# A triangular inverse on four quarters of TensorE's array, in pairs behind half units, and another order at the end of softmax

## The chip, the cores and the metric

The kernel runs on one core of a Trainium2 chip. The metric is the time of one execution on the device in microseconds (us), lower being better. Each engine (TensorE or PE, VectorE or DVE, ScalarE or ACT, GpSimd or POOL, SyncE or SP, which issues the weight DMAs) has its own queue and works it off in order. Engines wait for each other by semaphores.

## What is computed

One transformer block over 256 tokens of width 2048: a gated feed-forward, a mixer with two branches, and a second feed-forward, each with a layer norm. All is float32.

```
h = layer_norm(DEEPNORM_ALPHA * h + 0.5 * swiglu(h, ffn1_w_gate[l], ffn1_w_up[l], ffn1_w_down[l]), ...)
mix = hybrid_mixer(h, w_in[l], ...)
h = layer_norm(DEEPNORM_ALPHA * h + mix, ln2_g[l], ln2_b[l])
h = layer_norm(DEEPNORM_ALPHA * h + 0.5 * swiglu(h, ffn2_w_gate[l], ffn2_w_up[l], ffn2_w_down[l]), ...)
```

The mixer projects h by `w_in`. One branch is sparse attention: latent queries are projected by `w_q_idx` (for the index that picks 64 keys for each query) and by `w_uq` (for the attention), and softmax follows over the picked keys. The other is a gated delta rule over 8 heads in chunks of 64 tokens:

```
a_mat = jnp.where(strict, jnp.einsum('bhncd,bhned->bhnce', k_beta, k) * decay, 0.0)
m_mat = a_mat + jnp.eye(CHUNK, dtype=a_mat.dtype)
value = solve(v_beta)             # solve: a triangular solve with m_mat
k_cumdecay = solve(k_beta * jnp.exp(g_cum)[..., None])
```

The kernel solves by building the inverse of `m_mat`: 4 chunks of 64 tokens, 8 heads.

## The kernel before

**Units.** Every large product is cut into units: a 256 x 512 piece of a weight matrix. SP loads it into `raw` (8 slots), ACT rounds it into `whi` (`split_hi`, L351), DVE computes the rest into `wlo` (`split_lo`, L358), and `unit_mm` on PE multiplies with both. `whi` and `wlo` have 3 slots; a slot is free when the semaphore `unit_used` says that PE has finished the unit that used it, and PE raises `unit_used` behind the unit's last matmul only. ACT and DVE split unit w+2 while PE is at unit w. With the slot order of `ring_place`, which turns back in the second half of a product's units so that the next product finds its slots in order, the 8 units of `w_q_idx` take slots 0, 1, 2, 0, 1, 0, 1, 2 and the 4 of `w_uq` slots 0, 1, 2, 1. So units 5 and 6 take the slots of units 3 and 4, and unit 11 that of unit 9: these splits can only start when the unit two before them is finished.

**The latent query stage.** 12 units (w = 0 to 11) of 24 matmuls at L393, L395, L397, moving 256 columns each. A unit has two halves of 12 matmuls, one for each bank of `acc0`. Behind every second unit ACT evicts `acc0` into `qidxT` or `qT` (L1308).

**The inverse.** A tile has 128 partitions, and each of the two tiles of 128 tokens (t = 0, 1) holds two chunks, one on partitions 0 to 63 (`UPPER`), one on 64 to 127 (`LOWER`). The inverse Y and its transpose X grow over five levels: `t1_mm` (L1952) multiplies a level's part of the matrix with X, ACT evicts it to `t1` (L1317); `y_mm` (L1965) multiplies `t1` with Y, DVE subtracts it from Y (`yinv`, L1644, at level 5 into `yfull`, L1648); `x_mm` (L1978) transposes Y into X, ACT evicts it to `xinv` (L1321). A sixth step (L1955, L1968) joins the two chunks of a tile. Each of the steps is one *group* for each t: 8 heads x 2 chunks = 16 matmuls of 64 x 64, which the profile shows as 32 records, since a float32 matmul is two passes. A matmul whose operands are on `UPPER` and whose output is on `UPPER` uses one quarter of the 128 x 128 array, `LOWER` to `LOWER` the opposite one. The other two quarters are not used. The groups run as `items_behind(w)` between units: six (t1, y and x of a level, both t) behind each of the units 1, 3, 5 and 7, four each behind 8 and 9, two behind 10. `split_hi` and `split_lo` stand ahead of an even unit's groups and behind an odd unit's. PSUM: X and t1 in `acc1`, Y's product in two banks of `tp`.

**Behind it** come the index scores, the choice of 64 keys on DVE, the softmax on DVE and ACT (`logits`, `select`, `exps`, `normalise`), and beside it on PE the products of the delta rule: `vnew0`, `nkcd` (evicted by DVE, L1751), the state, o0 (L2095, which waits for `nkcd`'s eviction, since it overwrites its bank and the state's later product reads it), `vnew1`, then the attention's outputs `oT` (L2121 to L2123, one head after another through four banks; head h waits until `oT_lo` has read head h-4, L1784), then the units of `w_out`.

Of the kernel before, what the change touches and what calls it, by code (L numbers as in the profile page):

```python
# [19 lines left out]
P = 128  # L20
# [91 lines left out]
def hybrid_block(nc, x, x_t, ffn1_w_gate, ffn1_w_up, ffn1_w_down, ln1_g, ln1_b, w_in, q_norm_g, kv_norm_g,  # L112
# [52 lines left out]
    with ExitStack() as ctx:  # L165
# [209 lines left out]
        def unit_mm(pe, p, it, u, acc, free, n_chunk, moving, stat, kt0, first, last, a_done=None):  # L375


            n = st.phases[p].units
            s = ring_place(u, n, SPLIT_SLOTS)
            pe.wait_ge(lo_done, st.index(p, it, u + 1))  # L380
            for half in range(2):
                if first and n_chunk is not None:
                    wait(pe, free[half], n_chunk)
                if moving == "w":
                    ins = token_mm(pe, p, it, u, acc, half, stat, kt0, first, last)
                else:
                    for c in range(2):
                        cols = slice((2 * half + c) * P, (2 * half + c) * P + P)
                        o = acc[:, half, c * S:c * S + S]
                        for k in range(UNIT_KT):  # L390
                            hi, lo = stat[:, kt0 + k, 0, :], stat[:, kt0 + k, 1, :]
                            end = last and k == UNIT_KT - 1
                            pe.matmul(o, whi[:, s, k, cols], hi, start=first and k == 0 and c == 0,  # L393
                                      stop=False, skip_group_check=True)
                            pe.matmul(o, whi[:, s, k, cols], lo, start=False, stop=False,  # L395
                                      skip_group_check=True)
                            ins = pe.matmul(o, wlo[:, s, k, cols], hi, start=False, stop=end,  # L397
                                            skip_group_check=True)
                if half == 0 and last and a_done is not None:
                    ins.then_inc(a_done, 1)  # L400
            ins.then_inc(unit_used, 1)
# [514 lines left out]
        QUARTERS = (UPPER, LOWER)  # L916
        NAMES = ["xa", "ax", "spl", "sp", "beta", "tb", "g", "eg", "ekd", "gc", "rq", "rk",
# [45 lines left out]
        def x_bank(t):  # L963
            return acc1[:, t]

        def y_bank(t):
            return tp[:, t]
# [11 lines left out]
        def items_behind(w):  # L979
            return range(*{1: (0, 6), 3: (6, 12), 5: (12, 18), 7: (18, 24), 8: (24, 28), 9: (28, 32), 10: (32, 34)}.get(w, (0, 0)))  # L980

        def y_ups(lvl, t):

            done = T * (lvl - 1) + t + 1
            return done + (t + 1 if lvl == LEVELS else T if lvl > LEVELS else 0)
# [175 lines left out]
        def mixer_act(act):  # L1161
# [129 lines left out]
            def x_first(t):  # L1291

                act.wait_ge(sem("x0_ps"), t + 1)
                act.activation(xinv[:, t], heads8(x_bank(t)), ACT.Copy).then_inc(sem("x0"), 1)

            x_first(0)
            for w in range(LATENT_UNITS):
                p, u = latent_stage(w)
                if w % 2 == 0:
                    split_hi(act, p, 0, u + LEAD)  # L1300
                if u % QU == QU - 1:
                    j, dst = u // QU, (qidxT if p == WQI else qT)
                    for half in range(2):
                        if half == 0:
                            act.wait_ge(acc0a_done, n0[p] + j + 1)
                        else:
# [3 lines left out]
                if w == 0:  # L1310
                    x_first(1)
                for m in items_behind(w):
                    lvl, kind, t = item(m)
                    if kind == 0:
                        act.wait_ge(sem("t1_ps"), T * (lvl - 1) + t + 1)
                        rows = slice(0, P) if lvl <= LEVELS else LOWER
                        act.activation(t1[rows, t], heads8(x_bank(t)[rows]), ACT.Copy).then_inc(sem("t1"), 1)  # L1317
                    if kind == 2:
                        act.wait_ge(sem("x_ps"), T * (lvl - 1) + t + 1)
                        rows = slice(0, P) if lvl < LEVELS else UPPER  # L1320
                        act.activation(xinv[rows, t], heads8(x_bank(t)[rows]), ACT.Copy).then_inc(sem("x_up"), 1)  # L1321
# [53 lines left out]
            act.wait_ge(sem("o_out"), 1)  # L1375
            act.activation(o_squares[:, 0], o_first[:], ACT.Square).then_inc(sem("o_sq"), 1)
# [20 lines left out]
            for h in range(AH):  # L1397
                oT_hi(h)
                if h == 5:
                    act.wait_ge(sem("o_sum"), 2)  # L1400
                    act.activation(o_squares[:, 1], o_second[:], ACT.Square).then_inc(sem("o_sq"), 1)
# [27 lines left out]
        def mixer_dve(dve):  # L1429
# [203 lines left out]
            for w in range(LATENT_UNITS):  # L1633
                p, u = latent_stage(w)
                if w % 2 == 0:
                    split_lo(dve, p, 0, u + LEAD)
                if w == 0:
                    qk_times_decay(3)
                for m in items_behind(w):
                    lvl, kind, t = item(m)  # L1640
                    if kind == 1:
# [4 lines left out]
                        elif lvl == LEVELS:  # L1646
                            for rows in QUARTERS:
                                dve.tensor_tensor(yfull[rows, t, :, rows], yinv[rows, t], heads8(y_bank(t)[rows]),  # L1648
                                                  ALU.subtract).then_inc(sem("y_up"), 1)
# [3 lines left out]
                if w % 2:  # L1653
                    split_lo(dve, p, 0, u + LEAD)
# [63 lines left out]
            def select(i):  # L1718
# [6 lines left out]
                   .then_inc(sem("att_sel"), 1)  # L1725
                dve.wait_ge(sem("att_sel"), i + 1)
                dve.reduce_max(amax[:, t, heads], prob, AX_X).then_inc(sem("att_max"), 1)
                dve.wait_ge(sem("att_max"), i + 1)
# [67 lines left out]
            o_mean_square(0)  # L1796
            second_queries(2)
# [3 lines left out]
            for h in range(4):  # L1801
                oT_lo(h)
# [3 lines left out]
            for h in range(4, AH):  # L1806
                oT_lo(h)
            dve.wait_ge(sem("o_sum"), 2)
# [23 lines left out]
        def mixer_pe(pe):  # L1832
# [98 lines left out]
            def x_first(t):  # L1931
# [3 lines left out]
                for h in range(BH):  # L1935
                    for rows in QUARTERS:
                        ins = pe.matmul(x_bank(t)[rows, cols64(h)], yinv[rows, t, h], ident[rows, rows],
# [3 lines left out]
            def t1_mm(lvl, t):  # L1941
# [3 lines left out]
                if lvl == 1:  # L1945
                    pe.wait_ge(sem("x0"), t + 1)
                else:
                    pe.wait_ge(sem("x_up"), T * (lvl - 2) + t + 1)
                for h in range(BH):
                    if lvl <= LEVELS:  # L1950
# [3 lines left out]
                    else:  # L1954
                        ins = pe.matmul(x_bank(t)[LOWER, cols64(h)], aT[UPPER, t, h, LOWER], xinv[UPPER, t, h],  # L1955
# [3 lines left out]
            def y_mm(lvl, t):  # L1959

                pe.wait_ge(sem("t1"), T * (lvl - 1) + t + 1)
                for h in range(BH):
# [9 lines left out]
            def x_mm(lvl, t):  # L1972

                pe.wait_ge(sem("y_up"), y_ups(lvl, t))
                for h in range(BH):
                    if lvl < LEVELS:
                        for rows in QUARTERS:
                            ins = pe.matmul(x_bank(t)[rows, cols64(h)], yinv[rows, t, h], ident[rows, rows],  # L1978
                                            start=True, stop=True)
                    else:  # L1980
                        ins = pe.transpose(x_bank(t)[UPPER, cols64(h)], yfull[UPPER, t, h, UPPER], ident[UPPER, UPPER])
# [23 lines left out]
            for w in range(LATENT_UNITS):  # L2005
                p, u = latent_stage(w)
                j = u // QU
                unit_mm(pe, p, 0, u, acc0, acc0_free, n0[p] + j, "x", cqT, 2 * (u % QU), u % QU == 0, u % QU == QU - 1,
                        acc0a_done)
                if w == 0:  # L2010
                    x_first(1)
                for m in items_behind(w):
                    lvl, kind, t = item(m)
                    (t1_mm, y_mm, x_mm)[kind](lvl, t)
# [231 lines left out]
```

## Time and profile before

| | |
|---|---|
| median of 3 runs | 1948.9 us (1948.44 to 1949.24) |
| the profiled execution, its own time | 1949.24 us |
| its span | 1947.4 us |
| latent query stage (first matmul at L393 with `cqT` to first score matmul) | 989.34 to 1059.45 us |
| from the scores to the first unit of `w_out` | 1059.45 to 1113.02 us |

A matmul's record starts when the array takes it; its duration holds a latency of some 0.2 us in which others run, so the distance from start to start is what PE needs. A row with "x64" is a run of 64 records; its start and the start of the next row give the run's time. "Idle before <- who" is the time in which an engine had nothing in flight and who ended it. PE can look busy while it loses time: a late start of 0.1 to 0.2 us is hidden under the latency of the record ahead.

### The profile page before, as it was taken

To read this page: it belongs to the slowest core of one execution; us is meant where nothing else is said; L and a number is where in the kernel's file an instruction comes from. 1 tells how busy PE (TensorE), PEld (TensorE's weight loads), DVE (VectorE), ACT (ScalarE), POOL (GpSimd) and SP (SyncE) were. 2 spreads that over 40 slices of the span, in tenths; PEclk is the share of its full clock that TensorE was granted. 3 is DMA by queue.
4 is the path that set the end of the run, shared out by engine and by line. 5 is a ranking of instruction groups with operands and counts; after the bars stand their busy time and mean duration, and the time that the engine had idled before them with its cause. 6 is when DMAs were issued, how large, how long until landed. Compare 5 with 4: busy or idle time off the path is not lost.

```text
span 1947.4 us, 28504 instructions
## 1 busy us (share of the span) xinstructions
PE 1930.1 (99%) x10574; PEld 1642.7 (84%) x10574; DVE 1090.7 (56%) x1237; ACT 840.0 (43%) x934; POOL 64.1 (3%) x93
## 2 busy tenths in 40 slices
PE   9999999999999999999999999999999999999997
PEld 7888888888888888999999888888888888888886
DVE  5554554555454457667755957554555555544445
ACT  4444443444333343555645534444444444433332
POOL 0000000000000001300131100000000000000000
PEclk9999999999999999999999999999999999999999
DMA  8666666566665575664432057566666666555663
GB/s 295 191 189 189 191 185 187 180 191 212 212 200 190 192 247 135 211 190 149 134 122 88 23 203 261 165 188 187 180 187 202 185 193 185 190 168 192 204 203 142
DMA packets 185326, 357.28 MB, mean 183 GB/s; under 512 B 11296, under 2 KB 23584, under 8 KB 184240
## 3 DMA queue, kind: packets, MB, share of 16 engines
q1 hardware_dynamic: 183568, 347.43, 57.5%
q0 software_dynamic: 1696, 8.99, 1.4%
q8 instruction: 43, 0.70, 0.1%
q14 instruction: 19, 0.16, 0.0%
HBM read 354.28 MB, written 2.10 MB: 183 GB/s over the span
## 4 chain that ended last, share of the span: by engine, by line
PE 96%; DVE 2%; issue 1%; ACT 0%; DMA 0%; SPq 0%; POOL 0%; POOLq 0%; DVEq 0%; ACTq 0%
PE acc L370 27%; PE acc L372 27%; PE acc L371 27%; PE acc L393 3%; PE acc L397 3%; PE acc L395 3%; PE tp L732 1%; PE acc L1952 1%; PE tp L1965 0%; PE acc L1978 0%; PE tp L456 0%; DMA raw<-in_ffn_w_up_dram 0%; DVE work L1695 0%; DVE score L1681 0%; ACT whi L351 0%
## 5 line engine op out<-in xcount | busy, mean ns | idle before, releaser
L358 DVE TENSOR_TENSOR wlo<-raw,whi 128x1024 fp32r<-128x1024 f32 (+2 forms) x637 | 762.3, 1204 | 770.5 <-ACT whi L351 769.4
L351 ACT ACTIVATE whi<-raw 128x1024 fp32r<-128x1024 f32 (+2 forms) x637 | 656.4, 1039 | 938.0 <-PE acc L372 873.9
L370 PE MATMUL acc<-whi,xT 128*128 128x512 f32 (+2 forms) x1652 | 633.8, 384 | 2.6 <-DVE wlo L358 1.8
L372 PE MATMUL acc<-whi,xT 128*128 128x512 f32 (+2 forms) x1652 | 629.0, 381 | 0.0
L371 PE MATMUL acc<-wlo,xT 128*128 128x512 f32 (+2 forms) x1652 | 628.5, 380 | 0.0
L370 PEld LDWEIGHTS acc<-whi,xT 128*128 128x128 f32 x1652 | 310.2, 188 | 67.3 <-DVE wlo L358 2.7
L372 PEld LDWEIGHTS acc<-whi,xT 128*128 128x128 f32 x1652 | 310.2, 188 | 59.4
L371 PEld LDWEIGHTS acc<-wlo,xT 128*128 128x128 f32 x1652 | 310.4, 188 | 56.2
L370 PE MATMUL acc<-whi,hT 128*128 128x512 f32 x656 | 256.4, 391 | 0.0
L372 PE MATMUL acc<-whi,hT 128*128 128x512 f32 x656 | 255.4, 389 | 0.0
L371 PE MATMUL acc<-wlo,hT 128*128 128x512 f32 x656 | 255.3, 389 | 0.0
L370 PEld LDWEIGHTS acc<-whi,hT 128*128 128x128 f32 x656 | 123.1, 188 | 28.9 <-DVE resid L832 1.8
L372 PEld LDWEIGHTS acc<-whi,hT 128*128 128x128 f32 x656 | 123.2, 188 | 25.9
L371 PEld LDWEIGHTS acc<-wlo,hT 128*128 128x128 f32 x656 | 123.2, 188 | 24.7
L393 PE MATMUL acc<-xT,whi 128*128 128x256 f32 x384 | 108.7, 283 | 0.0
L395 PE MATMUL acc<-xT,whi 128*128 128x256 f32 x384 | 108.7, 283 | 0.0
L397 PE MATMUL acc<-xT,wlo 128*128 128x256 f32 x384 | 108.7, 283 | 0.0
L395 PEld LDWEIGHTS acc<-xT,whi 128*128 128x128 f32 x384 | 73.7, 192 | 0.0
L397 PEld LDWEIGHTS acc<-xT,wlo 128*128 128x128 f32 x384 | 73.7, 192 | 0.0
L393 PEld LDWEIGHTS acc<-xT,whi 128*128 128x128 f32 x384 | 73.7, 192 | 0.0
L657 POOL DMA_DIRECT2D ln_g<-in_ln_g_dram x3 | 1.9, 641 | 1431.8 <-PE acc L372 1431.8
L351 ACT ACTIVATE edge<-raw 128x1024 fp32r<-128x1024 f32 (+1 forms) x30 | 30.1, 1034 | 14.0 <-PE acc L372 11.6
(296 smaller groups left out, 1243.8 us busy)
## 6 DMA issues: line engine op xcount, KB each, us to landing
raw<-in_ffn_w_up_dram SPq DMA_DIRECT2D x176, 512.0 KB, 3.8
raw<-in_ffn_w_down_dram SPq DMA_DIRECT2D x176, 512.0 KB, 4.5
raw<-in_ffn_w_gate_dram SPq DMA_DIRECT2D x175, 512.0 KB, 3.8
raw<-in_w_in_dram SPq DMA_DIRECT2D x48, 512.0 KB, 4.0
raw<-in_w_out_dram SPq DMA_DIRECT2D x32, 512.0 KB, 6.5
raw<-in_w_in_dram SPq DMA_DIRECT2D x32, 260.0 KB, 2.8
raw<-in_w_in_dram SPq DMA_DIRECT2D x16, 456.0 KB, 5.2
raw<-in_w_q_idx_dram SPq DMA_DIRECT2D x8, 512.0 KB, 4.1
```

The source lines that it names most:

```text
L351: act.activation(hi[:, s, :, 0:w], raw[:, r, :, 0:w], ACT.Copy).then_inc(hi_done, 1)
L358: dve.tensor_tensor(lo[:, s, :, 0:w], raw[:, r, :, 0:w], hi[:, s, :, 0:w].bitcast(F32), ALU.subtract).then_inc(lo_done, 1)
L370: pe.matmul(o, hi, w_hi[:, s, k, 0:width], start=first and k == 0, stop=False)
L371: pe.matmul(o, hi, w_lo[:, s, k, 0:width], start=False, stop=False)
L372: ins = pe.matmul(o, lo, w_hi[:, s, k, 0:width], start=False, stop=last and k == UNIT_KT - 1)
L393: pe.matmul(o, whi[:, s, k, cols], hi, start=first and k == 0 and c == 0, stop=False, skip_group_check=True)
L395: pe.matmul(o, whi[:, s, k, cols], lo, start=False, stop=False, skip_group_check=True)
L397: ins = pe.matmul(o, wlo[:, s, k, cols], hi, start=False, stop=end, skip_group_check=True)
L657: pool.dma_start(dst[:], src.to_broadcast([P, D])).then_inc(sem("ln_gains"), 16)
L732: ins = pe.transpose(tp[:, k // 2, (k % 2) * S + t * P:(k % 2) * S + t * P + P], gated[:, t, k * P:k * P + P], ident[:])
L1952: ins = pe.matmul(x_bank(t)[rows, cols64(h)], lev[rows, t, h], xinv[rows, t, h], start=True, stop=True)
```

## The change

1. Four quarters. For heads 4 to 7 the output of `t1_mm` and `x_mm` goes to the other half of the partitions (`quarter_pairs`, `across`): t1 and Y of these heads live crossed, and x comes back. Of each four matmuls in a row, each uses another quarter. X's and t1's outputs now take two banks each (`x_at`: heads 0 to 3 in one, 4 to 7 in the other) in the four banks of `tp`, Y's product goes to `acc1`. `y_mm` still uses two quarters, as does the first transpose; the sixth step uses one.
2. To start, ACT copies heads 4 to 7 of Y crossed (for each t, one 128 x 256 copy and two of 64 x 256). At level 5 DVE writes `yfull` in 8 pieces of 64 x 256 instead of 4 of 64 x 512.
3. The groups go in pairs (both t of one step) behind each half of a unit: 17 pairs, from the second half of unit 1 to the second half of unit 9, 9 of them behind a unit and 8 in its middle.
4. `split_hi` and `split_lo` stand ahead of the groups in every unit, ACT's evictions of `acc0` one in each half.
5. DVE: `nkcd`'s eviction ahead of the last four `logits`; o's mean square (tile 0) behind `oT_lo` of head 5, the sums for `o_second` ahead of `oT_lo`. ACT: the squares of `o_first` behind `oT_hi` of head 1.
The queues of SP and POOL hold the same instructions in the same order as before.

```diff
+        def x_at(t, rows, h):
+            return tp[rows, 2 * t + h // CROSSED, (h % CROSSED) * HALF:(h % CROSSED) * HALF + HALF]
...
+        def items_behind(w, half):
+
+            pair = 2 * w + half - 3
+            return range(T * pair, T * pair + T) if 0 <= pair < ITEMS // T else ()
...
+        def quarter_pairs():
+
+            for k in range(CROSSED):
+                for h, crossed in ((k, False), (CROSSED + k, True)):
+                    for rows in QUARTERS:
+                        yield h, rows, across(rows) if crossed else rows
...
             for w in range(LATENT_UNITS):
                 p, u = latent_stage(w)
-                if w % 2 == 0:
-                    split_hi(act, p, 0, u + LEAD)
-                if u % QU == QU - 1:
-                    j, dst = u // QU, (qidxT if p == WQI else qT)
-                    for half in range(2):
+                split_hi(act, p, 0, u + LEAD)
+                if w == 0:
+                    x_first(1)
+                for half in range(2):
+                    if u % QU == QU - 1:
...
-                if w % 2:
-                    split_hi(act, p, 0, u + LEAD)
...
-                        for rows in QUARTERS:
-                            ins = pe.matmul(x_bank(t)[rows, cols64(h)], lev[rows, t, h], xinv[rows, t, h],
-                                            start=True, stop=True)
...
+                    for h, rows, to in quarter_pairs():
+                        ins = pe.matmul(x_at(t, to, h), lev[rows, t, h], xinv[rows, t, h], start=True, stop=True)
...
-            logits(1, range(AH // 2, AH))
             for b in range(2):
                 dve.wait_ge(sem("nkcd_ps"), b + 1)
                 dve.tensor_scalar(nkcdT[:, 4 * b:4 * b + 4, :], heads4(acc0[:, b]), -1.0, None, ALU.mult)\
                    .then_inc(sem("nkcd"), 1)
+            logits(1, range(AH // 2, AH))
```

PE behind units 1 and 2, before: t1, y and x of level 1 stand in one block behind unit 1 (`t_90` is `t1`).

```order
L397 MATMUL acc<-cqT,wlo 128x256
L1952 MATMUL acc<-xinv,lev 64x64 [waits s_x0,s_lev]
L1952 MATMUL acc<-xinv,lev 64x64 x15
L1952 MATMUL acc<-xinv,lev 64x64 [waits s_x0,s_lev]
L1952 MATMUL acc<-xinv,lev 64x64 x15
L1965 MATMUL tp<-yinv,t_90 64x64 [waits s_t1]
```

After, the same y groups stand in the middle of unit 2 (L1995), with the unit's second half right behind them; its first row waits for the second bank of `acc0`.

```order
L398 MATMUL acc<-cqT,wlo 128x256
L1995 MATMUL acc<-yinv,t_90 64x64 [waits s_y_cross,s_t1]
L1995 MATMUL acc<-yinv,t_90 64x64 x15
L1995 MATMUL acc<-yinv,t_90 64x64 [waits s_y_cross,s_t1]
L1995 MATMUL acc<-yinv,t_90 64x64 x15
L394 MATMUL acc<-cqT,whi 128x256 [waits s_acc0b_free]
```

Each step's groups moved away from each other, by one half unit.

ACT around unit 3, before: the groups of level 2 (`t1`, then `xinv`) stand ahead of the split of unit 5 (`s_raw_loaded5`).

```order
L351 ACTIVATE whi<-raw 128x1024 [waits s_unit_used,s_raw_loaded4]
L1329 ACTIVATE thz<-zab 128x512 [waits s_acc0a_free]
L1308 ACTIVATE qidxT<-acc 128x512 [waits s_acc0a_done]
L1308 ACTIVATE qidxT<-acc 128x512 [waits s_unit_used]
L1317 ACTIVATE t_90<-acc 128x512 [waits s_t1_ps] x2
L1321 ACTIVATE xinv<-acc 128x512 [waits s_x_ps] x2
L351 ACTIVATE whi<-raw 128x1024 [waits s_unit_used,s_raw_loaded5]
```

After, units 3 and 4:

```order
L351 ACTIVATE whi<-raw 128x1024 [waits s_unit_used,s_raw_loaded5]
L1339 ACTIVATE qidxT<-acc 128x512 [waits s_acc0a_done]
L1348 ACTIVATE t_90<-tp 128x512 [waits s_t1_ps] x2
L1339 ACTIVATE qidxT<-acc 128x512 [waits s_unit_used]
L1358 ACTIVATE thz<-zab 128x512 [waits s_z,s_acc0b_free]
L351 ACTIVATE whi<-raw 128x1024 [waits s_unit_used,s_raw_loaded6]
L1352 ACTIVATE xinv<-tp 128x512 [waits s_x_ps] x2
L1348 ACTIVATE t_90<-tp 128x512 [waits s_t1_ps] x2
```

The splits of units 5 and 6 moved ahead of the evictions of the groups that run inside units 3 and 4.

DVE at softmax's end, before:

```order
L1729 TENSOR_SCALAR nmax<-amax 128x4 [waits s_att_max]
L1713 SCALAR_TENSOR_TENSOR prob_107<-ndist,tp 128x256 [waits s_att_ps] x4
L1751 TENSOR_SCALAR nkcdT<-acc 128x512 [waits s_nkcd_ps] x2
L1737 RECIPROCAL pinv<-psumm 128x8 [waits s_prob_exp]
L1739 TENSOR_TENSOR prob_106<-prob_106,pinv 128x1024 [waits s_pinv]
```

After:

```order
L1758 TENSOR_SCALAR nmax<-amax 128x4 [waits s_att_max]
L1779 TENSOR_SCALAR nkcdT<-acc 128x512 [waits s_nkcd_ps] x2
L1742 SCALAR_TENSOR_TENSOR prob_107<-ndist,tp 128x256 [waits s_att_ps] x4
L1766 RECIPROCAL pinv<-psumm 128x8 [waits s_prob_exp]
L1768 TENSOR_TENSOR prob_106<-prob_106,pinv 128x1024 [waits s_pinv]
```

`nkcd`'s eviction moved ahead of four logits; the rest of the queue around it is the same.

## Rows read from the trace of the kernel before

**Rows 1.** The page, part 1: busy us, share of the span, instructions.
```profile
PE 1930.1 (99%) x10574; PEld 1642.7 (84%) x10574; DVE 1090.7 (56%) x1237; ACT 840.0 (43%) x934; POOL 64.1 (3%) x93
```
**Rows 2.** Busy times of the latent stage: span, PE, PEld, DVE, ACT, POOL, clock.
```profile
989.34:1059.45 70.11, 69.83 (x1299) 67.87 (x1297) 31.25 (x38) 33.36 (x50) 12.40 (x11) 1.00 0.26 85
```
**Rows 3.** Groups of instructions, PE, whole kernel: count, busy us, mean ns.
```profile
L1952 PE MATMUL acc<-xinv,lev 64*64 64x64 f32 x320 | 10.4, 220 | 0.0
L1978 PE MATMUL acc<-ident,yinv 64*64 64x64 f32 x256 | 8.3, 220 | 0.0
```
**Rows 4.** Timeline of PE, one block of six groups: start, us, instruction.
```profile
996.46 0.28 PE L397 MATMUL acc<-cqT,wlo 128*128 128x256 f32 x1
996.66 2.08 PE L1952 MATMUL acc<-xinv,lev 64*64 64x64 f32 x64
998.58 2.03 PE L1965 MATMUL tp<-yinv,t 64*64 64x64 f32 x64
1000.47 2.08 PE L1978 MATMUL acc<-ident,yinv 64*64 64x64 f32 x64
1002.48 0.39 PE L393 MATMUL acc<-cqT,whi 128*128 128x256 f32 x1
1002.71 0.28 PE L395 MATMUL acc<-cqT,whi 128*128 128x256 f32 x1
```
**Rows 5.** Timeline of PE: the sixth step (one quarter), and its wait.
```profile
1048.08 1.08 PE L1981 MATMUL acc<-ident,yfull 64*64 64x64 f32 x16
1049.39 2.08 PE L1955 MATMUL acc<-xinv,aT 64*64 64x64 f32 x32 [0.23 <-ACT xinv L1321]
```
**Rows 6.** Windows of 20 ns at the start of a two-quarter and a one-quarter run.
```profile
996.66:996.68 0.02, 0.02 (x3) 0.02 (x2) 0.00 (x0) 0.00 (x0) 0.00 (x0) 1.00 1.84 717
1049.38:1049.40 0.02, 0.01 (x1) 0.01 (x1) 0.00 (x0) 0.02 (x1) 0.00 (x0) 1.00 0.00 0
```
**Rows 7.** Timeline of PEld: loads of 128 columns ahead of matmuls of 16 columns.
```profile
945.80 0.30 PEld L1869 LDWEIGHTS tp<-small,up_to 128*128 128x128 f32 x2
946.02 0.30 PEld L1869 LDWEIGHTS tp<-small,later 128*128 128x128 f32 x2
```
**Rows 8.** Timeline of ACT: the split of unit 6 behind unit 4's end.
```profile
1017.57 1.06 ACT L351 ACTIVATE whi<-raw 128x1024 fp32r<-128x1024 f32 x1 [1.05 <-PE acc L397]
```
**Rows 9.** Timeline of PE: the end of unit 4 and the start of unit 5.
```profile
1017.19 0.28 PE L397 MATMUL acc<-cqT,wlo 128*128 128x256 f32 x1
1017.31 0.39 PE L393 MATMUL acc<-cqT,whi 128*128 128x256 f32 x1
1017.53 0.28 PE L395 MATMUL acc<-cqT,whi 128*128 128x256 f32 x1
```
**Rows 10.** Timeline of ACT behind a split and a wait: starts of neighbours.
```profile
1003.09 1.05 ACT L351 ACTIVATE whi<-raw 128x1024 fp32r<-128x1024 f32 x1
1004.04 0.62 ACT L1329 ACTIVATE thz<-zab 128x512 f32<-128x512 f32 x1
1048.18 0.60 ACT L1308 ACTIVATE qT<-acc 128x512 f32<-128x512 f32 x1 [0.84 <-PE acc L397]
1048.75 1.07 ACT L1321 ACTIVATE xinv<-acc 64x512 f32<-64x512 f32 x2
```
**Rows 11.** Timelines of DVE and PE around the eviction of nkcd.
```profile
1093.49 1.41 DVE L1713 SCALAR_TENSOR_TENSOR prob<-ndist,tp 128x256 f32<-128x256 f32 x4
1094.82 1.28 DVE L1751 TENSOR_SCALAR nkcdT<-acc 128x512 f32<-128x512 f32 x2
1092.72 1.95 PE L2089 MATMUL acc<-vnew,ktok 128*128 128x128 f32 x16
1095.56 2.05 PE L2095 MATMUL acc<-vnew,aiT 128*128 128x128 f32 x16 [0.89 <-DVE nkcdT L1751]
```
**Rows 12.** Timelines of PE and DVE around head 4 of oT.
```profile
1109.67 0.39 PE L2123 MATMUL tp<-pT,vatt 128*128 128x128 f32 x2
1110.32 0.46 PE L2121 MATMUL acc<-pT,vatt 128*128 128x128 f32 x2 [0.26 <-DVE xT L1784]
```

More of the change, by code:

```diff
@@ L373, in token_mm, with unit_mm @@
             return ins
-        def unit_mm(pe, p, it, u, acc, free, n_chunk, moving, stat, kt0, first, last, a_done=None):
+        def unit_mm(pe, p, it, u, acc, free, n_chunk, moving, stat, kt0, first, last, a_done=None,
+                    behind_half=None):
             n = st.phases[p].units
@@ L400, in unit_mm @@
                     ins.then_inc(a_done, 1)
+                if half == 0 and behind_half is not None:
+                    behind_half(0)
             ins.then_inc(unit_used, 1)
@@ L977, in hybrid_block, with across @@
         LATENT_UNITS = (QI_CHUNKS + UQ_CHUNKS) * QU
-        def items_behind(w):
-            return range(*{1: (0, 6), 3: (6, 12), 5: (12, 18), 7: (18, 24), 8: (24, 28), 9: (28, 32), 10: (32, 34)}.get(w, (0, 0)))
+        def items_behind(w, half):
+            pair = 2 * w + half - 3
+            return range(T * pair, T * pair + T) if 0 <= pair < ITEMS // T else ()
         def y_ups(lvl, t):
             done = T * (lvl - 1) + t + 1
-            return done + (t + 1 if lvl == LEVELS else T if lvl > LEVELS else 0)
+            return done + 3 * (t + 1 if lvl == LEVELS else T if lvl > LEVELS else 0)
+        def across(rows):
+            return LOWER if rows is UPPER else UPPER
+        def quarter_pairs():
[3 more added lines that the diff above has]
+                        yield h, rows, across(rows) if crossed else rows
         def mixer_loads(sp):
@@ L1291, in x_first @@
             def x_first(t):
+                last = slice(CROSSED, BH)
+                act.wait_ge(sem("y0"), t + 1)
+                act.wait_ge(sem("qk_ps"), 4)
+                act.activation(t1[:, t, last], yinv[:, t, last], ACT.Copy).then_inc(sem("x0"), 1)
                 act.wait_ge(sem("x0_ps"), t + 1)
-                act.activation(xinv[:, t], heads8(x_bank(t)), ACT.Copy).then_inc(sem("x0"), 1)
+                act.activation(xinv[:, t], heads8(y_bank(t)), ACT.Copy).then_inc(sem("x0"), 1)
+                act.wait_ge(sem("x0"), 2 * t + 1)
+                for rows in QUARTERS:
+                    act.activation(yinv[across(rows), t, last], t1[rows, t, last], ACT.Copy).then_inc(sem("y_cross"), 1)
             x_first(0)
@@ L1309, in mixer_act @@
                                        ACT.Copy).then_inc(acc0_free[half], 1)
[L1310 to L1321, printed above, removed]
-                if w % 2:
-                    split_hi(act, p, 0, u + LEAD)
+                    for m in items_behind(w, half):
+                        lvl, kind, t = item(m)
+                        if kind == 0:
+                            act.wait_ge(sem("t1_ps"), T * (lvl - 1) + t + 1)
+                            if lvl == 1:
+                                act.wait_ge(sem("y_cross"), 2 * t + 2)
+                            rows = slice(0, P) if lvl <= LEVELS else LOWER
+                            act.activation(by_bank(t1[rows, t]), x_all(t, rows), ACT.Copy).then_inc(sem("t1"), 1)
+                        if kind == 2:
+                            act.wait_ge(sem("x_ps"), T * (lvl - 1) + t + 1)
+                            rows = slice(0, P) if lvl < LEVELS else UPPER
+                            act.activation(by_bank(xinv[rows, t]), x_all(t, rows), ACT.Copy).then_inc(sem("x_up"), 1)
                 if 1 <= w < 5:
@@ L1800, in mixer_dve @@
                .then_inc(sem("o_sum"), 1)
-            for h in range(4):
-                oT_lo(h)
+            second_queries(2)
             dve.wait_ge(sem("o_out"), 3)
@@ L1805, in mixer_dve @@
             dve.tensor_tensor(o_second[:], o_second[:], o_state[:], ALU.add).then_inc(sem("o_sum"), 1)
-            for h in range(4, AH):
+            for h in range(6):
                 oT_lo(h)
-            dve.wait_ge(sem("o_sum"), 2)
+            o_mean_square(0)
+            for h in range(6, AH):
+                oT_lo(h)
             o_mean_square(1)
@@ L1974, in x_mm @@
                 pe.wait_ge(sem("y_up"), y_ups(lvl, t))
[L1975 to L1981, printed above, removed]
+                if lvl < LEVELS:
+                    for h, rows, to in quarter_pairs():
+                        ins = pe.matmul(x_at(t, to, h), yinv[rows, t, h], ident[rows, rows], start=True, stop=True)
+                else:
+                    for h in range(BH):
+                        ins = pe.transpose(x_at(t, UPPER, h), yfull[UPPER, t, h, UPPER], ident[UPPER, UPPER])
                 ins.then_inc(sem("x_ps"), 1)
```

64 lines of the change are left out of this document (35 added, 29 removed).

## The prediction

> **What bounds the kernel now.** I read the page's busy times first: PE 99% of the span, DVE 56%, ACT 43% [rows 1]. So only what shortens PE's own work or its waits moves the end. The windows of the latent stage say the same for the place of the change: 70.11 us with PE busy 69.83, DVE 31.25 and ACT 33.36, the clock at 1.00, its higher level [rows 2]. Then the timeline of PE there, reading distances from start to start. A plain matmul of a unit needs 0.12 us. 64 records of t1 need 1.92 us and 64 of y 1.89, about 29.5 ns a record [rows 4]. The sixth step, which uses one quarter, needs the 2.08 us of such a run for 32 records, where t1 has 64 in it [rows 4, 5]: one quarter works at 58.5 ns a record, and two quarters at exactly double rate. Last, the rows where PE waits: for `xinv` in the sixth step, for `nkcd` (0.89 us idle) and for `oT_lo` (0.26 idle) [rows 5, 11, 12].
>
> **Four quarters.** t1 has 320 records and x 256 [rows 3], 576 together. If four quarters work side by side as two do, the record's share falls from 29.2 ns (58.4 by two) to 14.6: 576 x 14.6 ns = **-8.4 us**. No row shows two quarters on the same partitions at once (`UPPER` to `UPPER` and `UPPER` to `LOWER`). The bounds are 0 (they take turns) and -8.4. For the gain: in the first 20 ns of a t1 run two weight loads have started, where the one-quarter run has one [rows 6], so the second quarter starts within 20 ns, and the queue that feeds the array isn't the limit at 29 ns. Against it: 128 columns of weights need 0.11 us a load even where only 16 columns are streamed (two loads in 0.22 us) [rows 7], so 64 columns need about as long as a record lasts; if the quarters of one half of the rows share the path of the weights, they take turns. I take -8.4, since two quarters show no loss at all.
>
> The row shows that inside one quarter a load runs under the matmul ahead of it: 58.5 ns a record, where load and stream one after the other would need about 107 [rows 5, 7]. The Trainium skill, TensorE: Matmul & The Clock Gate, section Part 3: Packing small matmuls, says that a weight load overlaps running matmuls only where the row group differs. By that rule, quarters on the same rows would take turns and this term would be 0; within a quarter the trace does not agree with it.
>
> **More stops.** Entering the small matmuls costs 0.20 us from the last 0.12 us matmul instead of 0.12, the first run is 0.03 to 0.05 longer than the second, and the exit adds 2.01 - 1.89 = 0.12 [rows 4]: 0.25 us a stop. 17 stops instead of 7: +2.5. Behind the exit the second matmul comes after 0.23 us instead of 0.12; a unit's start has this anyway [rows 9], but the 8 stops inside a unit may pay it anew, 0 to 0.8; I take 0.4. **+2.9**, from +2.5 to +3.3.
>
> **Waits inside the stage.** The stop for `xinv` (1049.39 - 1048.08 = 1.31 us for a run that needs 16 x 0.056 = 0.90) goes, since half a unit, 1.44 us, now lies between the steps: **-0.4**. That half unit also covers ACT's two evictions (0.60 each, starting 0.49 to 0.57 apart [rows 10]), DVE's two subtractions, the crossed copies and `yfull` in 8 pieces: each of these pairs is done about 1.2 us behind its PE run, or (8 pieces of 64 x 256, by half the 64 x 512 piece's time) about at the moment PE asks. Taken as 0; if the cover fails, 0.3.
>
> **The splits ahead of the evictions.** Here the change adds a wait. The split of unit 6 takes unit 4's slot and can't start before unit 4 is finished: PE's last matmul of unit 4 starts at 1017.19, so the unit ends at 1017.31, and ACT, idle for 1.05 us, starts the split at 1017.57 [rows 8, 9]. Before, nothing stands behind it that PE needs. Now groups run inside units 3, 4 and 9, and the splits of units 5, 6 and 11 (whose slots those units free) stand at the head of ACT's queue there. Queued behind them is the eviction of the groups behind the first half; PE asks for it right behind the second half.
> - Unit 3: from its end 0.26 us until the split, 0.95 until ACT's next instruction [rows 10], 0.49 for the eviction of `acc0` (a pair takes 1.07, so the second starts 0.48 behind the first), 0.60 for t1 of tile 0, 0.06 to PE: 2.36 us; PE would have started after 0.09. Stall 2.27.
> - Unit 4 has no eviction of `acc0` (even): xinv of tile 0 at 0.26 + 0.95 + 0.60 + 0.06 = 1.87. Stall 1.78.
> - Unit 9: as unit 3, 2.27. The other splits wait for a unit already finished.
> **+6.3 us**. It can't be hidden: PE has nothing else in its order. DVE's split behind ACT's (1.2 us) is done before y's product is. The stage thus comes to -8.4 + 2.9 - 0.4 + 6.3 = **+0.4**.
>
> **Softmax's end.** `nkcd`'s first half is evicted from 1094.82 on; PE would be free at 1092.72 + 16 x 0.112 = 1094.51 and starts at 1095.56 [rows 11]. With the four logits (1.33 us) behind it, the eviction runs from 1093.49 and its second half is done at about 1094.8, before head 4 asks for it. Gain 1.05. Next in line for PE are the state's eviction (ACT) and `prob`, both there before PE asks, by 0.1 us or more. At head 4 of oT 1110.32 - 1109.67 = 0.65 us lie where 0.22 would do [rows 12]: gain up to 0.43, as the mean square (1.5 us) leaves `oT_lo`'s way. But the sums for `o_second` now stand ahead of `oT_lo` and may cost 0.1. Later work of `w_out` keeps its cover. **-1.4**, from -1.0 to -1.5. SP's and POOL's queues don't change.
>
> **The sum.** +0.4 - 1.4 = -1.0 us. The profiled execution, 1949.24 us (span 1947.4 and 1.84 around it), becomes 1948.2; it stands 0.3 above the median, so the forecast is **1947.9 us** against 1948.9. A measurement of this kernel can tell 0.2%, 3.9 us, from no change.
>
> **The rivals.**
> 1. The quarters on the same rows take turns (slower). Place: the nine pairs of t1 and x groups. Price: the 8.4 us don't come, so 1947.9 + 8.4 = **1956.3**. For it: the load time [rows 7]; against it: the clean doubling [rows 4, 5]. The change is slower by over 3.9 us from the point at which a record of these groups needs more than 14.6 + (3.9 + 1.0) / 0.576 = 23 ns.
> 2. A part only: starts on the array can't come closer than some limit between 14.6 and 29.2 ns; at the middle, 1947.9 + 4.2 = **1952.1**. Two starts within 20 ns are shown, four are not [rows 6]. The same page of the Trainium skill (section Wait — 56ns, not 53.3ns?) has a floor of about 25 ns from start to start; by it the time would be 1947.9 + 576 x 10.4 ns = 1953.9. Two loads within 20 ns speak against it where the quarters differ.
> 3. The change does better than its order says: the three stalls aren't there (the split finds a free slot, or ACT catches up), 1947.9 - 6.3 = **1941.6**. Against it: [rows 8], the same wait in the kernel before.
> 4. Worse: changing between two quarters of the same rows costs each time what entering costs (106 ns to the second record instead of 58, the 0.05 of [rows 4]): 8 changes in each of 18 groups x 0.05 = 7 us on top of rival 1, about **1963**. Or PE's stalls of 2.3 us bring the clock to its lower level; the wait of 1.05 us at [rows 11] left it at 1.00, and longer ones aren't in these stages.
>
> **How the numbers follow.** Forecast 0.55, rival 1 0.20, rival 2 0.10, rival 3 0.08, rival 4 0.07. The forecast and rival 2's better half stay within 0.2%; rivals 1 and 4 and the worse half of 2 are slower, rival 3 is faster. Faster 0.08, same 0.60, slower 0.32. The forecast's own range, from its terms, is 1946.0 to 1949.0. The range for 8 in 10 takes in rivals 1 and 2 and leaves out 3 and 4: 1945.0 to 1957.5.
>
> **What would show it.** In the timeline of PE after: 64 records of t1 in 0.94 us (right) or 1.9 (rival 1); the x runs likewise, y still 1.89. Idle time of PE of some 2 us ended by ACT's `t` ahead of y behind unit 3 and behind unit 9, and by `xinv` ahead of t1 behind unit 4, with ACT's split starting 0.26 us behind each of these units' ends; if they are missing, the step on the splits was wrong. The o0 run starting right behind the state's products, and head 4 of oT with less than 0.3 us. The whole is wrong above all if the quarters of the same rows take turns.

## The result, and the profile after

The changed kernel needs **1953.6 us** (median of 20 executions, 1951.9 to 1955.4) against 1948.9 (1948.1 to 1950.0): a ratio of 1.0023, 95% interval 1.0017 to 1.0029. It is slower by 4.8 us; the likeliest case of the prediction was 1.0 us faster. The profiled execution took 1953.78 us, with a span of 1951.7.

The page's busy times hardly differ from those of before [rows 1]: PE is busy for 0.1 us less, in a span that is 4.3 us longer. First the page, part 1, of the changed kernel:

```profile
PE 1930.0 (99%) x10574; PEld 1640.0 (84%) x10574; DVE 1090.9 (56%) x1241; ACT 840.5 (43%) x940; POOL 64.9 (3%) x93
```

The window of the latent stage, from the same matmul to the same matmul as in [rows 2] (span; PE, PEld, DVE, ACT, POOL busy; granted clock; DMA share; GB/s):

```profile
988.96:1064.85 75.89, 68.97 (x1298) 64.83 (x1297) 31.71 (x42) 33.67 (x54) 13.22 (x11) 0.93 0.30 99
```

The stage became 5.78 us longer (70.11 before), where the prediction had +0.4. Two things differ: PE is idle for 6.9 us of it instead of 0.3, and the granted clock is 0.93 instead of 1.00. From the first matmul of the scores to the first of `w_out` it is 1.57 us less (52.00, before 53.57); the rest, 1823.8 us against 1823.7, is as it was.

**The array works as forecast.** Timeline of PE around the first t1 run (start, us, instruction), to be laid beside [rows 4]:

```profile
996.08 0.28 PE L398 MATMUL acc<-cqT,wlo 128*128 128x256 f32 x1
996.29 1.16 PE L1980 MATMUL tp<-xinv,lev 64*64 64x64 f32 x64
997.38 0.39 PE L394 MATMUL acc<-cqT,whi 128*128 128x256 f32 x1
997.60 0.28 PE L396 MATMUL acc<-cqT,whi 128*128 128x256 f32 x1
```

From the first of the 64 records to the unit's next matmul it is 1.09 us. A y run, which still uses two quarters, needs 2.01 from start to exit: 0.92 us less for 64 records is a gain of 14.4 ns for each. What a record still costs follows from the run's own row: 1.16 us less the 0.22 of its last record, over 63 steps, is 14.9 ns, and for a y run (2.08 us) by the same working 29.5.

**The three stalls are there, at the forecast places, and something else behind two of them.** Timeline of PE at the ends of units 3, 4 and 9 (in brackets: idle time before, and what ended it):

```profile
1007.88 0.28 PE L398 MATMUL acc<-cqT,wlo 128*128 128x256 f32 x1
1010.34 3.41 PE L1995 MATMUL acc<-yinv,t 64*64 64x64 f32 x64 [2.18 <-ACT t L1348]
1013.68 0.57 PE L394 MATMUL acc<-cqT,whi 128*128 128x256 f32 x1
...
1020.05 1.18 PE L1980 MATMUL tp<-xinv,lev 64*64 64x64 f32 x64 [1.78 <-ACT xinv L1352]
...
1051.43 0.28 PE L398 MATMUL acc<-cqT,wlo 128*128 128x256 f32 x1
1054.01 2.82 PE L1998 MATMUL acc<-yfull,t 64*64 64x64 f32 x32 [2.31 <-ACT t L1348]
1056.76 0.58 PE L394 MATMUL acc<-cqT,whi 128*128 128x256 f32 x1
1057.14 0.41 PE L396 MATMUL acc<-cqT,whi 128*128 128x256 f32 x1
1057.36 0.41 PE L398 MATMUL acc<-cqT,wlo 128*128 128x256 f32 x1
```

The same y run that needs 2.01 us elsewhere takes 3.34 behind unit 3's stall, and behind unit 9's the matmuls of a unit start 0.22 us apart where 0.12 is usual. That is the clock. Windows of the stalls and of what follows them (the number behind POOL's is the granted clock):

```profile
1008.00:1010.30 2.30, 0.16 (x2) 0.00 (x0) 0.95 (x1) 2.04 (x4) 0.70 (x1) 1.00 0.00 0
1010.30:1013.70 3.40, 3.36 (x65) 3.25 (x65) 0.96 (x2) 1.48 (x3) 0.00 (x0) 0.56 0.00 0
1018.00:1020.05 2.05, 0.27 (x3) 0.09 (x2) 0.59 (x1) 1.68 (x3) 0.00 (x0) 1.00 0.00 0
1020.05:1051.40 31.35, 30.75 (x679) 28.70 (x680) 14.52 (x22) 13.66 (x22) 5.75 (x4) 1.00 0.17 53
1051.40:1054.00 2.60, 0.31 (x3) 0.10 (x1) 1.11 (x1) 2.17 (x4) 0.00 (x0) 1.00 0.00 0
1054.00:1061.90 7.90, 7.89 (x56) 7.77 (x57) 3.21 (x5) 1.99 (x3) 1.47 (x2) 0.57 0.80 278
```

Behind the stalls of units 3 and 9 (PE idle for 2.18 and 2.31 us) the clock is at its lower level, 1.2 GHz, while PE works at full load. Behind unit 4's (1.78) it stays at 1.00. PE counts as busy in these windows, which is why the page's busy time shows nothing of the loss.

ACT's timeline says why PE stood still; it is the queue that the prediction describes, split, eviction of `acc0`, eviction of t1:

```profile
1008.26 1.06 ACT L351 ACTIVATE whi<-raw 128x1024 fp32r<-128x1024 f32 x1 [3.24 <-PE acc L398]
1009.22 0.58 ACT L1339 ACTIVATE qidxT<-acc 128x512 f32<-128x512 f32 x1
1009.70 1.08 ACT L1348 ACTIVATE t<-tp 128x512 f32<-128x512 f32 x2
```

One shorter wait is new too, behind unit 8, ahead of the second tile of the last transpose. Timelines of PE and of DVE, whose eight pieces of `yfull` PE is waiting for:

```profile
1044.60 0.63 PE L2010 MATMUL tp<-ident,yfull 64*64 64x64 f32 x8
1045.82 0.63 PE L2010 MATMUL tp<-ident,yfull 64*64 64x64 f32 x8 [0.59 <-DVE yfull L1678]
...
1042.20 3.56 DVE L1678 TENSOR_TENSOR yfull<-yinv,acc 64x256 f32<-64x256 f32 x8
```

**Softmax's end is as forecast.** Timelines of PE and DVE, beside [rows 11, 12]: the o0 run (L2127) starts right behind the state's products, 16 x 0.11 us behind 1098.10, and head 4 of oT 0.26 us behind its neighbour instead of 0.65.

```profile
1098.10 1.95 PE L2121 MATMUL acc<-vnew,ktok 128*128 128x128 f32 x16
1099.88 1.28 PE L2127 MATMUL acc<-vnew,aiT 128*128 128x128 f32 x10
...
1098.87 1.28 DVE L1779 TENSOR_SCALAR nkcdT<-acc 128x512 f32<-128x512 f32 x2
...
1113.93 0.39 PE L2155 MATMUL tp<-pT,vatt 128*128 128x128 f32 x2
1114.19 0.46 PE L2153 MATMUL acc<-pT,vatt 128*128 128x128 f32 x2
```

**The spread fits this.** The 20 executions of the changed kernel fall into groups by the mean granted clock of the whole execution:

```
mean clock   executions   us
0.997        8            1951.92 to 1952.52
0.996        8            1953.28 to 1954.36
0.995        4            1954.38 to 1955.38
```

The profiled execution, which has both low stretches, is of the middle group; where the four of 0.995 had more, no trace tells. Of the kernel before, 80 executions stood beside the later kernels on three chips: 78 have 0.998 or 0.999, two have 0.997 (1950.30 and 1950.87 us).

### The profile page after: what moved, and what is told of

Read it like the earlier page. It is cut to its first block, busy times and chain, and to the rows that moved or that the text cites. A ratio compares the mean times of both kernels' runs of the same rounds, so it can differ in the third digit from the quotient of the medians.

```text
span 1951.7 us, 28519 instructions
## 1 busy us (share of the span) xinstructions
PE 1930.0 (99%) x10574; PEld 1640.0 (84%) x10574; DVE 1090.9 (56%) x1241; ACT 840.5 (43%) x940; POOL 64.9 (3%) x93
## 4 chain that ended last, share of the span: by engine, by line
PE 97%; DVE 1%; issue 1%; ACT 1%; DMA 0%; SPq 0%; POOLq 0%; POOL 0%; DVEq 0%; ACTq 0%
PE acc L370 27%; PE acc L372 27%; PE acc L371 27%; PE acc L394 3%; PE acc L396 3%; PE acc L398 3%; PE tp L735 1%; PE tp L2057 1%; PE acc L1995 0%; PE tp L459 0%; PE acc L2066 0%; PE acc L2085 0%; DVE wlo L358 0%; DMA raw<-in_ffn_w_up_dram 0%; ACT whi L351 0%
```

## The experiments

Theory A: the parts of the change are worth what the prediction says, and the miss is the clock, which falls because PE stands still behind units 3 and 9. Its rivals: the four quarters themselves lower the clock or cost something elsewhere; or the miss is a cost of the 17 stops. Kernels named in one paragraph ran on the same chip unless it says otherwise; where chips differ, only the ratios to the kernel before on that chip are compared.

**late_splits: the splits behind the groups.** Only the place of three pairs of instructions differs from the changed kernel:

```diff
+        LATE = (3, 4, 9)
...
-                split_hi(act, p, 0, u + LEAD)
+                if w not in LATE:
+                    split_hi(act, p, 0, u + LEAD)
...
+                if w in LATE:
+                    split_hi(act, p, 0, u + LEAD)
```

DVE's `split_lo` likewise.

> The changed kernel with one thing undone: in the units 3, 4 and 9 ACT's and DVE's splits stand behind the groups again, so the evictions of t1 and xinv don't queue behind a split that waits for the unit's end. Theory A (the stalls of 2.4, 2.0 and 2.5 us that the changed kernel's trace shows come from the splits' place, and the clock fell because of them: 5 us more): both go, 1953.6 - 6.3 - 5 = about 1942.3 us, clock at 1.00 through the stage. Theory B (the clock falls because the 64 x 64 groups now spread over the stage and half of them run in half the time, not because of the stalls): the stalls go, the low clock stays, 1953.6 - 6.3 = about 1947.3 us. Theory C (ACT is late anyway): no change, 1953.

Measured: **1942.5 us** (1942.27 to 1942.96), 0.9972 of before (0.9961 to 0.9984; before 1948.0 on this chip). The stage takes 65.51 us, the clock is 1.00 in all of it:

```profile
988.85:1054.36 65.51, 64.48 (x1298) 60.50 (x1297) 31.68 (x42) 34.15 (x54) 12.91 (x11) 1.00 0.27 85
```

PE's order is the same as in the changed kernel, so the two traces can be laid on each other record by record. Timeline of late_splits at the end of unit 3, to be laid beside 1007.88, 1010.34 and 1013.68 above:

```profile
1007.77 0.28 PE L398 MATMUL acc<-cqT,wlo 128*128 128x256 f32 x1
1007.98 2.08 PE L2002 MATMUL acc<-yinv,t 64*64 64x64 f32 x64
1009.99 0.39 PE L394 MATMUL acc<-cqT,whi 128*128 128x256 f32 x1
```

The changed kernel falls behind by 2.24 us at unit 3's stall and by 1.49 in the low stretch behind it, by 1.87 at unit 4's, by 2.38 at unit 9's and by 2.98 in the low stretch behind that; 0.6 of it comes back between units 4 and 9, where late_splits has a wait behind unit 5 that the stall covers. Stalls 6.5, clock 4.5, less 0.6: 10.4 us, all within the stage.

**busy_stalls: the stalls stay, PE works in them.** The changed kernel with products of the identity matrix, whose result nothing uses, in front of the groups that PE waits for:

```diff
+        FILL = {3: 9, 4: 7, 9: 9}
...
+                for _ in range(FILL.get(w, 0)):
+                    pe.matmul(acc1[:, 0, 0:P], ident[:], ident[:], start=True, stop=True)
```

> The changed kernel with nothing moved, but PE multiplies the identity by itself (9, 7 and 9 matmuls of 0.22 us, into a bank that the next product overwrites) in the stalls behind the units 3, 4 and 9. They add no work that matters and take no wait away. Theory A (the stalls let the clock fall): the clock stays at 1.00 and the 5 us of its two low stretches go: 1953.6 - 5 = about 1948.6 us, just what my sum gave for the stage with its stalls and without a clock loss. Theory B (the groups let it fall): no gain, 1953.6 us or more, low stretches as before.

Measured, beside late_splits: **1948.65 us** (1947.89 to 1950.97), 1.0005 of before (0.9996 to 1.0014). PE's timeline and the windows at unit 3 show the wait as long as ever (its next y run starts 2.46 us behind the unit's last matmul), but filled:

```profile
1007.42 0.28 PE L398 MATMUL acc<-cqT,wlo 128*128 128x256 f32 x1
1007.54 2.17 PE L2048 MATMUL acc<-ident 128*128 128x128 f32 x18
1009.88 1.32 PE L1996 MATMUL acc<-yinv,t 64*64 64x64 f32 x38 [0.17 <-ACT t L1349]
...
1009.90:1013.30 3.40, 3.40 (x75) 3.33 (x76) 2.19 (x4) 1.42 (x3) 0.00 (x0) 1.00 0.02 5
```

The stage takes 71.40 us, 4.49 less than in the changed kernel and just the 4.5 that the alignment gives to the clock; it is 5.89 more than in late_splits, which is the stalls' 6.5 less 0.6. In the times the ratio's interval ends at 1.0014, where the changed kernel's begins at 1.0017. Added work made the kernel faster: the idle time of PE is what the low clock follows, and not the groups, their quarters or the stops, which are all still here.

**two_quarters: late_splits without the crossing** (`across` returns its argument, so all heads stay on their own half).

```diff
         def across(rows):
...
-            return LOWER if rows is UPPER else UPPER
+            return rows
```

> As late_splits, but no head is crossed: t1 and x use two quarters, everything else (pairs behind half units, banks, copies in the same number and size) is as it was. Theory A (four quarters double the rate of 576 records, 14.6 ns each): 8.4 us more than late_splits, about 1950.7 us. Rival (the place of the groups brought the gain, not the quarters): as late_splits. 64 records of t1 take 1.87 us instead of 0.94.

Measured, beside late_splits: **1949.85 us** (1948.85 to 1950.64), 1.0009 of before (1.0000 to 1.0018): 7.35 us slower than late_splits, a microsecond short of the 8.4. Its trace has hardly anything left of the two waits (0.66 and 0.81 us from start to start) that late_splits has behind units 5 and 8: its longer runs cover the first and all but 0.3 us of the second. best_two, below, settles this.

**softmax_only: the kernel before with the changed end of softmax alone** (item 5 of the change).

> The kernel before with the change's last part alone: nkcd's eviction ahead of the last four logits, the mean square behind oT_lo of head 5, the squares on ACT behind oT_hi of head 1. Theory: the wait for nkcd (1.05 us) and that of head 4 (0.43) go: 1948.9 - 1.4 = 1947.5 us. Rival (another wait takes their place, DVE's queue or ACT's): 1948.9.

Measured, on late_splits' chip: **1946.32 us** (1945.58 to 1947.08), 0.9991 of before (0.9982 to 1.0000), 1.65 us faster; its stretch from the scores to `w_out` is 52.04 us, before 53.57.

**stall3, stall4, stall9: one stall each.** late_splits with one of the three splits put back in front (`LATE = (4, 9)`, `(3, 9)` and `(3, 4)`). The three ran on one chip, where late_splits didn't run; its ratio (0.9972, and 0.9974 when it ran again) puts it at 1943.4 us there.

> late_splits (1942.5 us, no stall) with the split of unit 5 back ahead of the groups in unit 3: one stall of 2.3 us. Theory A (a stall of this length lets the clock fall by itself, as behind this stall in the changed kernel: 3.4 us at the lower level, 1.7 us lost): 1942.5 + 2.3 + 1.7 = 1946.5 us. Rival (it takes more than one stall within the stage): 1942.5 + 2.3 = 1944.8 us, clock at 1.00.

> late_splits with the split of unit 6 back ahead of the groups in unit 4: one stall of 1.8 us. In the changed kernel's trace the clock doesn't fall behind it. Theory A: 1942.5 + 1.8 = 1944.3 us, clock at 1.00. Rival (each stall costs the clock): about 1946.

> late_splits with the split of unit 11 back ahead of the groups in unit 9, where the sixth step's groups use one quarter of the array and PE waits 0.7 us more for DVE shortly before: one stall of 2.3 us. Theory A (the clock falls for 6.8 us as in the changed kernel, 3.4 us lost): 1942.5 + 2.3 + 3.4 = 1948.2 us. Rival: 1944.8 us. The three single stalls should add up to the 11.1 us between late_splits and the changed kernel, if each lets the clock fall on its own.

Measured, against 1948.66 of before:

```
kernel   median us  range               ratio (95%)               above 1943.4   stage us   stall in its trace
stall3   1946.98    1945.12 to 1947.62  0.9989 (0.9980, 0.9998)   3.6            67.73      2.24
stall4   1944.79    1944.29 to 1946.55  0.9982 (0.9973, 0.9992)   1.4            66.79      1.87, less 0.6 that it covers
stall9   1947.75    1945.45 to 1948.97  0.9995 (0.9986, 1.0004)   4.4            70.88      2.36
```

In the median stall4 costs its idle time and no more; three of its eleven executions have a mean clock of 0.997 and took 1945.4 to 1946.6 us, and their low stretches, wherever they lie, are in no trace. The other two cost 1.3 and 2.0 us beyond it in the median, and their ranges begin at about the price of the stall alone: stall9's two executions with a mean clock of 0.998 took 1945.45 and 1945.98 us, its seven with 0.997 took 1947.2 to 1948.7 and its two with 0.996 took 1948.7 and 1949.0. So the fall isn't certain. stall9's profiled execution has it behind unit 9, and its stage is 5.4 us longer than late_splits', 3.0 more than the stall. In stall3's the clock stays up behind the same 2.18 us idle (the stage is 2.2 us longer, the stall alone), and is low at another place, at the start of the kernel, behind a wait for one of the first splits. So what stall3 costs beyond its stall is not shown to come from unit 3. That this stall alone can be followed by the low clock shows in the changed kernel, where it is the first of the three. Windows of stall9, then of stall3 with PE's row at its start:

```profile
1046.30:1048.90 2.60, 0.29 (x4) 0.09 (x2) 1.14 (x1) 2.21 (x4) 0.00 (x0) 1.00 0.00 0
1048.90:1055.80 6.90, 6.90 (x48) 6.78 (x49) 3.18 (x5) 1.95 (x3) 1.47 (x2) 0.51 0.77 247
```

```profile
1009.90:1012.35 2.45, 0.27 (x3) 0.07 (x1) 0.99 (x1) 2.08 (x4) 0.81 (x1) 1.00 0.00 0
1012.35:1016.00 3.65, 3.65 (x79) 3.45 (x79) 2.21 (x4) 1.44 (x3) 0.00 (x0) 1.00 0.00 0
...
11.40:14.80 3.40, 3.40 (x10) 2.67 (x9) 2.93 (x4) 2.48 (x3) 0.00 (x0) 0.51 1.05 409
...
10.91 0.50 PE L370 MATMUL acc<-whi,xT 128*128 128x512 f32 x1 [1.89 <-DVE wlo L358]
```

The kernel before has that wait too, and the clock stayed up behind it in its profiled execution:

```profile
10.84 0.50 PE L370 MATMUL acc<-whi,xT 128*128 128x512 f32 x1 [1.75 <-DVE wlo L358]
...
11.40:14.80 3.40, 3.40 (x16) 2.82 (x15) 3.13 (x3) 2.59 (x4) 0.00 (x0) 1.00 1.05 408
```

**upper_first: late_splits with the pieces of `yfull` in the order in which they are read.**

```diff
-                            for rows in QUARTERS:
-                                for heads, to in ((slice(0, CROSSED), rows), (slice(CROSSED, BH), across(rows))):
+                            for to in QUARTERS:
+                                for heads, rows in ((slice(0, CROSSED), to), (slice(CROSSED, BH), across(to))):
```

The last transpose then waits only for the pieces that it reads, and the product that reads the others (L2007) waits for all of them.

> late_splits with the eight pieces of level 5's yfull in another order: for each t the two that the next transpose reads come first, and the transpose waits for these alone. In the changed kernel's trace PE stands 0.8 us between the two transposes where 0.06 would do. Theory: 0.6 us less than late_splits, 1941.9 us. Rival (DVE is late by its split): no change, 1942.5.

Measured, on the chip of the stalls: 1942.55 us (1941.82 to 1942.70), 0.9968 (0.9956 to 0.9980), 0.0005 below late_splits' ratios; the wait behind unit 8 is gone from the trace, and the stage takes 64.72 us instead of 65.51.

**late_again, best, best_two, latent_only**, on one chip. best is upper_first with DVE's split of unit 5's turn behind y's subtraction as well (the wait that this removes is behind unit 5, not in its middle as the expectation has it), best_two is best without the crossing, latent_only is the changed kernel with softmax's end as before.

```diff
-                if w not in LATE:
+                if w not in (*LATE, 5):
                     split_lo(dve, p, 0, u + LEAD)
```

> The same kernel as late_splits, run again as the yardstick for the three beside it. It measured 0.9972 of the kernel before (1942.5 us there); expected again 0.997 to 0.9975 of the kernel before on this chip, with the granted clock at its higher level all through the latent stage.

> late_again with its two remaining short waits of PE taken away: the eight pieces of yfull come in the order in which they are read (the gap of 0.81 us ahead of the last transpose becomes 0.15 or less), and DVE's split of the unit behind unit 5 stands behind y's subtraction instead of ahead of it (the gap of 0.66 us in the middle of unit 5 becomes 0.2). Theory A (both waits lie on PE's path): 0.65 + 0.45 = 1.1 us faster than late_again. Rival B (another wait of the same length is next in line behind each): the same time as late_again.

> The kernel best with the crossing taken out: all eight heads stay on their own half of the partitions, so t1 and x use two quarters of the array instead of four, all else alike. Theory A (the four quarters are worth 576 x 14.6 ns, and late_splits against two_quarters showed 7.35 us only because PE lost 1.1 us of it to the two waits that longer runs cover): 8.4 us slower than best. Rival B (the quarters cost about 1 us of their own somewhere else, for instance at the entry): 7.3 us slower than best.

> The changed kernel with softmax's end in the order of the kernel before: only the latent stage's part of the change. If the parts add up (softmax_only measured 0.9991 of the kernel before, the whole change 1.0023), it stands at 1.0032 of the kernel before, 6.2 us above it, with the clock at its lower level behind stalls as in the whole change. If the softmax part's gain depends on the stage ahead of it, it is elsewhere than 1.0027 to 1.0037.

Measured, against 1948.59 of before (1947.81 to 1949.38):

```
kernel        median us  range               ratio (95%)               stage us   scores to w_out
late_again    1943.35    1942.78 to 1946.09  0.9974 (0.9965, 0.9984)   65.47      52.02
best          1942.08    1941.44 to 1942.49  0.9965 (0.9951, 0.9979)   64.13      52.01
best_two      1950.27    1949.45 to 1950.87  1.0008 (0.9999, 1.0017)   72.41      52.01
latent_only   1954.21    1952.15 to 1956.07  1.0027 (1.0016, 1.0037)   75.90      53.55
```

best is 1.3 us below late_again (1.1 expected), the fastest version here and 6.5 us below the kernel before. Its stage is full to the last tenth: span 64.13, PE busy 64.08.

```profile
989.29:1053.42 64.13, 64.08 (x1298) 60.38 (x1297) 31.68 (x42) 33.86 (x54) 12.92 (x11) 1.00 0.27 87
```

best_two is 8.2 us slower than best, 8.28 in the stages (8.4 expected): the missing microsecond of two_quarters was the two waits (its stage is 0.3 us longer than best_two's, late_splits' 1.4 longer than best's). latent_only is 5.6 us above the kernel before, where 6.2 was expected; with softmax_only's -1.65 that makes +4.0 for the whole change, which measured +4.8 elsewhere. The parts add up within what these runs can tell. In latent_only's profiled execution the clock is low again behind units 3 and 9 (0.59 in the 3.30 and the 7.22 us behind their stalls) and not behind unit 4. latent_only's trace shows both waits of [rows 11, 12] again:

```profile
1100.71 1.49 PE L2127 MATMUL acc<-vnew,aiT 128*128 128x128 f32 x11 [0.89 <-DVE nkcdT L1779]
...
1115.47 0.46 PE L2153 MATMUL acc<-pT,vatt 128*128 128x128 f32 x2 [0.26 <-DVE xT L1812]
```

## Why the prediction was wrong

- **Four quarters, -8.4: right.** 8.2 to 8.3 us (best_two against best). Rivals 1 and 2 fall with it. The two rules of the Trainium skill that spoke for them don't hold here: TensorE: Matmul & The Clock Gate, Part 3: Packing small matmuls, has a weight load overlap running matmuls only where the row group differs, and the section Wait — 56ns, not 53.3ns? has a floor of about 25 ns from start to start; a record of these runs takes 14.9 ns, though of each four in a row every one shares its rows with another.
- **More stops, +2.9: right.** best_two's stage is 2.30 us above before's, with four quarters, stalls and short waits all out of it. With the 0.4 that left with the wait for `xinv` (by [rows 5]) the ten stops cost 2.7.
- **The cover of half a unit, taken as 0: too small.** "About at the moment PE asks" was judged for `yfull`, and 0.3 was named if it failed. DVE needs 3.56 us for both tiles' pieces, and the second tile's transpose waited for all eight, though it reads only two of its tile's four, the first and the last, which upper_first writes first: 0.8 us in the stage (65.51 against 64.72). A second wait of 0.4 to 0.6 us, behind unit 5 for y's subtraction, was hidden in the changed kernel by the stall ahead of it.
- **The stalls, +6.3: right**, to the engine and the tile: 2.24, 1.87 and 2.38, together 6.5 us, against 2.27, 1.78 and 2.27.
- **Softmax's end, -1.4: right.** -1.57 in the profile, -1.65 in the medians.
- **The clock: this is the step that failed.** The sum holds the stalls at the price of their idle time alone. That they could bring the clock down was named, as the second half of rival 4, with a chance of 0.07 shared with another mechanism and without a time of its own, on the ground that a wait of 1.05 us (0.89 of it idle) had left it at 1.00. Such a row says little of three waits that the same text makes 1.8 to 2.3 us long. The kernel's start has a nearer row, 1.75 us idle with the clock up behind it, and that wouldn't have been enough either: the same wait, 1.89 us long, is followed by the low clock in stall3. It was a cost that no row of before bounds from above, so it belonged in the sum as a term with two ends. At half speed for as long as it lasted here it cost 4.5 us in the profiled execution.

The time lies in the range of 1945.0 to 1957.5, but only because rivals 1 and 2 had stretched it, and they are the ones that the runs refute.

With the measured terms the stage comes out: -8.3 + 2.7 - 0.4 + 0.8 + 6.5 + 4.5 = +5.8, and 5.78 was measured. The clock is 4.5 of the 5.4 us that the prediction missed there. Over all executions its share is less sure: the changed kernel stands at 1.0023 and busy_stalls, which keeps its waits but did not run beside it, at 1.0005. That is 3.5 us, from one ratio that is known to 1.2 us and one that is known to 1.8. The eight executions with a mean clock of 0.997 may have had one fall only; no trace of one was kept.

Open is what decides whether a wait of some 2 us is followed by the lower clock. In the traces it follows all three stalls of 2.31 us (changed kernel, latent_only, stall9), two of the three of 2.18 (not in stall3), none of the three of 1.78 (changed kernel, latent_only, stall4), and at the kernel's start the wait of 1.89 but not that of 1.75. No run here tells more.

## What to carry to other kernels

Before a change sends PE idle for a couple of microseconds at once, price the stretch behind the wait too: the busy time doesn't show it, only the granted clock of the windows behind each stall and the distance between neighbouring matmuls do. An order in which a slot's refill stands in front of the eviction that PE needs next gives away everything that a faster array brought; behind the eviction the same refill cost nothing at these three places. When a part is made faster, look at which short waits its old length covered: two of them, 1.3 us, were worth nearly as much as the whole of softmax's end.

## What the hardware showed that wasn't expected

- Idle times of PE of 2.18 and 2.31 us were followed by matmuls at 1.2 GHz, for some 3 and 7 us, though PE was fully busy again: unit matmuls 0.22 instead of 0.12 us apart, a y run 3.34 instead of 2.01 us. PE's idle time itself was shown with a clock of 1.00.
- 25 products of no use in the stalls (50 records) kept the clock up; the stage was 4.49 us shorter with them.
- Four 64 x 64 quarters at once work at about twice the rate of two, the pairs on the same rows included: 14.9 ns a record against 29.5.
